# Attention scores from high and low parts: three fp32r products in place of one fp32 product

## The chip, the core and the metric

The kernel runs on one core of a Trainium2 chip. The metric is device time in microseconds (us), the median of three runs. The engines are TensorE (PE in the profile; PEld is its loading of weights), VectorE (DVE), ScalarE (ACT), GpSimd (POOL) and SyncE (SP), which here only issues transfers. Each engine works through its own list of instructions in order, and waits on semaphores for the others.

## The reference

Two layers are computed over 256 + 512 = 768 tokens (a prompt and a sample, which do not see each other) of width 1024. In each layer a projection `h @ w_in` feeds two mixers with four heads each: a gated linear attention (HGRN2, called gla in the kernel) and a differential attention. Their outputs go through a projection, a convolutional feed-forward part and a gated embedding. The change is in the scores of the differential attention:

```
q = apply_rope(q, cos, sin) * (DA_DH ** -0.5)      # DA_DH = 64, two maps m per head
k = apply_rope(k, cos, sin)
def block(q_blk):                                  # 128 queries
    s = jnp.einsum('bhmqd,bhmkd->bhmqk', q_blk, k).astype(jnp.float32)
    p = jax.nn.softmax(s, axis=-1)
    a = p[:, :, 0] - lam * p[:, :, 1]
    return jnp.einsum('bhqk,bhkv->bhqv', a.astype(v.dtype), v)
```

## The kernel before

All data are fp32. The large products (projections, feed-forward) are already made as three fp32r products: an operand x is split into a high part, which ACT writes by a copy from fp32 to fp32r, and a low part, x minus high, which DVE writes, and PE adds high x high, high x low and low x high in PSUM (`PASSES = ((0, 0), (0, 1), (1, 0))`). The small products of the two mixers are plain fp32 products.

Every engine's order is written out by hand; a `Steps` object counts named steps on a semaphore, and `done(...)` or `wait_ge(...)` waits for one. A head of both mixers is one pass `it` (eight passes: 0 to 3 in the first layer, 4 to 7 in the second). In `mixers(L, h)` PE goes through seven levels k of the gla; between them stand the attention of query block k (`att_scores`, `att_turn_weights`, `att_values`) and pieces of the projection that fill the time (`side(s)`; the table `SLOTS` says how many eighths of a projection unit stand at each place s).

Six query blocks q make a pass. Blocks 0 and 1 belong to the prompt and meet 256 keys, blocks 2 to 5 meet 512. A head has two maps m of 64 features each. Map 0 lies on partitions 0 to 63 of the tile QK, map 1 on 64 to 127, so a score step is two products of 64 rows, into two PSUM banks. QK holds queries (index 0) and keys (index 1) of all 768 tokens; QKs is a copy with the halves exchanged, for the rotation (rope). DVE makes the rotated QK in three steps of 1536 columns: `cqk` and `sqk` (multiplications, L1743) and `radd` (their sum, L1740).

The turn from one head to the next is where the change's new steps stand. PE ends the gla output of pass `it` (L1021), goes through `side(TAIL + 2)` (lines L1088), the first gla step of the next pass (L942) and the scores of its block 0 (L1041), then `side(TAIL + 3)`, then transposes of the gla output (L1027), then `side(TAIL + 4)`. `SLOTS` gives these three places 2, 0, 2 eighths after heads 0 and 2, and 1, 1, 2 after head 1; there is no turn after head 3. Meanwhile ACT squares the gla output (L2697) and merges keys (L2448); DVE copies that output (L1727, L1729), sums the squares (L1731), waits for POOL, which makes the norm from them (`ms`, L2282, and the power `rs`, L2284), scales the output (step `on`, L1807), reduces the scores of block 0 (L1748) and makes the gla queries (L1678). PE's transposes L1027 wait for `on`. The chain that starts there goes on through the gated output (L1816), ACT's high part of the next weights (L2368), DVE's low part (L1509), the gla keys (L1691), to ACT's copy of the turned weights (L2653), for which PE's first value product L1060 of the pass waits.

At the start of a layer there is no such turn: block 0 of head 0 stands in the middle of projection unit 14, after its fourth eighth.

Of the kernel before, what the change touches and what calls it, by code (L numbers as in the profile page):

```python
# [22 lines left out]
P = 128  # L23
# [7 lines left out]
NH = 4  # L31
# [95 lines left out]
def view(ap, offset, dims):  # L127

    return bass.AP(tensor=ap.tensor, offset=ap.offset + offset, ap=[list(ap.ap[0])] + [list(d) for d in dims])
# [110 lines left out]
def att_names():  # L240

    act, dve, pe = ["nb0", "e0_0", "e0_1"], ["mx0", "rc0", "lr0", "al0"], ["sc0"]
    for k in range(NT + 1):
        if k + 1 < NT:
            pe += [f"sc{k + 1}"]
            dve += [f"{x}{k + 1}" for x in ("mx", "rc", "lr", "al")]
        pe += [f"tra{k}", f"av{k}"] if k < NT else []
        act += ([f"oc{k - 1}"] if k else []) + ([f"nb{k + 1}", f"e{k + 1}_0", f"e{k + 1}_1"] if k + 1 < NT else []) + ([f"at{k}"] if k < NT else [])
    pe += ["tro0", "tro1"]
    act += ["sq", "ab0", "ab1"]  # L250
    dve += ["ss", "on"]
    return act, dve, pe


def build(nc, x_in, p_in, w_in, lb_logits, gnorm, lam_in, subln, w_a, w_b, w_out, n_mix_pre, n_mix_post,
          w_up, conv_p, w_down, n_ffn_pre, n_ffn_post, w_ple, w_ple_gate, n_ple, ident_in, masks_in,
          rope_in, out):
    with ExitStack() as ctx:
# [84 lines left out]
        for l in range(1, NL + 1):  # L343
            totals.append((TOT, sum(2 * (T >> k) for k in range(1, l))))
        QK, QKs, PR, At = stack(x_off, h_off, [
            ("QK", [P, 2, T], F32), ("QKs", [P, 2, T], F32), ("PR", [P, 2, 2, TS], F32), ("At", [P, 2, TS], F32)])
        SQ2 = view(At[:], 0, [[P, NT], [1, P]])
        ab2 = view(O2[:], 0, [[1, T]])
        HN = put("HN", [P, KD, T], F32, m_off)[0]
# [78 lines left out]
        def steps(name, names, credit=False):  # L428
            return Steps(sem(name), names, len(names) if credit else 0)
# [13 lines left out]
        G_tro = steps("gla_turned", ["tro0", "tro1"])  # L443
        G_pool = steps("gla_pool", ["ms", "rs"])
        A_rope = steps("att_rope", ["cqk", "sqk", "radd"])
        ta, td, tp = att_names()
        A_act, A_dve, A_pe = steps("att_act", ta), steps("att_dve", td), steps("att_pe", tp)
        A_pool = steps("att_pool", ["ms", "rs"])
# [360 lines left out]
        def _(pe):  # L809
# [221 lines left out]
            def att_scores(it, q):  # L1031
                k0, kn = SEQ_OF[q]
                if q == 0:
                    pe.wait_ge(A_rope.sem, A_rope.at(it, "radd"))
                    if it:
                        pe.wait_ge(A_act.sem, A_act.at(it - 1, "ab1"))
                else:
                    pe.wait_ge(A_act.sem, A_act.at(it, f"e{q - 1}_1"))
                for m in range(2):
                    rows_ = slice(m * DA_DH, (m + 1) * DA_DH)  # L1040
                    ins = mm(ps[:, AB[m], 0:kn], QK[rows_, 0, q * P:(q + 1) * P], QK[rows_, 1, k0:k0 + kn], start=True, stop=True)  # L1041
                ins.then_inc(*A_pe.step(f"sc{q}"))

            def att_turn_weights(it, q):
# [412 lines left out]
        def _(dve):  # L1457
# [267 lines left out]
            def gla_output(it):  # L1725
                done(G_pe, it, "o")
                v.tensor_copy(O1[:, 0:4, :], view(ps[:], GB[0] * 512, [[P, 4], [1, P]])).then_inc(*G_out.step("o0"))  # L1727
                done(G_sq, it, "sq1")
                v.tensor_copy(O1[:, 4:NT, :], view(ps[:], GB[1] * 512, [[P, NT - 4], [1, P]])).then_inc(*G_out.step("o"))  # L1729
                done(G_sq, it, "sq")  # L1730
                v.tensor_reduce(st_g[:, 0, :], SQ1[:], AX_X, ALU.add).then_inc(*G_out.step("ss"))  # L1731

            def att_rope(it, L, n):
# [7 lines left out]
                else:  # L1741
                    src, tab = (QK, 0) if n == "cqk" else (QKs, T)
                    v.tensor_tensor(src[:], src[:], view(rope[:], tab, [[0, 2], [1, T]]), ALU.mult).then_inc(*A.step(n))  # L1743

            def att_max(it, n):
                A, p = A_dve, n % 2
                done(A_pe, it, f"sc{n}")
                v.tensor_reduce(mx[:, p, :], ps[:, AB[0]:AB[0] + 2, 0:SEQ_OF[n][1]], AX_X, ALU.max, negate=True).then_inc(*A.step(f"mx{n}"))  # L1748
# [16 lines left out]
            def mixers(L, h):  # L1765
# [4 lines left out]
                    for j in side_splits(h, s):  # L1770
                        low(unit(L, j))

                def att_first(it):
                    att_max(it, 0)
                    att_weights(it, 0)

                if h == 0:
                    att_first(it)
                side(PRE)
                for k in range(NL):  # L1780
                    level_up_keys(it, k)
# [19 lines left out]
                if following:  # L1801
                    gla_keys(it + 1)
                    att_rope(it + 1, L, "radd")
                gla_output(it)
                done(G_pool, it, "rs")
                done(G_out, it, "o")
                v.tensor_tensor(O1, O1, view(st_g[:], 2 * NT, [[1, NT], [0, P]]), ALU.mult).then_inc(*G_out.step("on"))  # L1807
# [15 lines left out]
            for L in range(DEPTH):  # L1823
# [57 lines left out]
                v.tensor_scalar(sl_col[:], sl_col[:], lay_now[:, 1:2], None, ALU.mult).then_inc(*lay_dve.step("slw"))  # L1881
                gla_forget(L * NH)
                gla_keys(L * NH)
                gla_queries(L * NH)
                low(unit(L, DENSE))
                for h in range(NH):
                    mixers(L, h)
                for c in range(KD):
# [468 lines left out]
        def _(act):  # L2357
# [98 lines left out]
            def att_exponentials(it, n):  # L2456
# [8 lines left out]
                for m in range(2):  # L2465
                    a(PR[:, p, m, 0:kn], ps[:, AB[m], 0:kn], ACT.Exp, bias=nb[:, p, m:m + 1], scale=DA_DH ** -0.5,
                      accum_out=sm[:, p, m:m + 1]).then_inc(*A_act.step(f"e{n}_{m}"))

            def exponential_table(it):
                if it:  # L2470
                    done(A_table, it - 1, "in")
                a(exp_ahead[:], half_neg[:, 0:1], ACT.Exp).then_inc(*A_table.step("in"))
# [144 lines left out]
            def mixers(L, h):  # L2617
# [78 lines left out]
                done(G_out, it, "o0")  # L2696
                a(SQ1[:, 0:4, :], view(ps[:], GB[0] * 512, [[P, 4], [1, P]]), ACT.Square).then_inc(*G_sq.step("sq"))  # L2697
                if following:
                    merge_keys(it + 1, 0)
                exponential_table(it)  # L2700
                side(TAIL + 2)
# [62 lines left out]
            for L in range(DEPTH):  # L2764
# [67 lines left out]
                in_copy(L, I1 - 1, "c21")  # L2832
                in_store_rest(L, I1 - 1)
                load_v(L, 0)
                high(unit(L, I1 + 1))
                copy_out(L, I1, 0, (0, 7))
                store_out(L, I1, 0)
# [499 lines left out]
```

## Time and profile before

| what | before |
|---|---|
| median of 3 runs | 2427.83 us (2427.82 to 2428.07) |
| profiled execution, from the first to the last instruction (span) | 2426.0 us |
| PE busy | 2413.1 us (99%) |
| PEld busy | 2251.7 us (93%) |
| DVE busy | 1825.9 us (75%) |
| ACT busy | 1302.4 us (54%) |
| POOL busy | 195.1 us (8%) |
| mean granted clock of TensorE | 0.999 of full speed |
| DMA, mean | 133 GB/s |

A matmul's record begins when PE takes it up and ends when its result is out, so records overlap, and a busy PE is not yet a PE at its peak; what a matmul costs in a row of them is the distance from start to start. The profile has only the span of its execution; the runs' median lies 1.83 us above it, for what comes before the first instruction and after the last.

### The profile page before, as it was taken

How to read it: one execution, taken by the hardware profiler on the slowest of the kernel's cores; microseconds unless marked ns; L12 is line 12 of the kernel's file. 1: busy time of each engine (PE TensorE's matmuls, PEld its weight loads, DVE VectorE, ACT ScalarE, POOL GpSimd, SP SyncE). 2: the span in 40 equal slices, each digit the busy share in tenths (PEclk: the TensorE clock that was granted, in tenths of full speed). 3: DMA queues.
4: the chain of work that ended last, by engine and by line, in shares of the span. 5: the costliest groups of instructions: out<-in, count | busy, mean ns of one | idle time of the engine just before them, and what ended most of it. 6: DMA issues, size and time to landing. Idle time of an engine off the chain costs nothing.

```text
span 2426.0 us, 40808 instructions
## 1 busy us (share of the span) xinstructions
PE 2413.1 (99%) x16410; PEld 2251.7 (93%) x16410; DVE 1825.9 (75%) x2403; ACT 1302.4 (54%) x2014; POOL 195.1 (8%) x236
## 2 busy tenths in 40 slices
PE   9999999999999999999999999999999999999998
PEld 9999989998999999888899998899989999998887
DVE  6666777754888998978585567777649889999784
ACT  6444666543555556556454456665436555554563
POOL 0001011100200000003110011011002000000031
PEclk9999999999999999999999999999999999999999
DMA  5454444344323233833233544343443232346421
GB/s 179 138 179 135 137 138 146 117 169 150 105 72 100 84 103 108 300 114 130 97 128 125 179 148 133 128 140 126 173 148 109 68 90 84 109 155 252 153 95 61
DMA packets 290411, 321.52 MB, mean 133 GB/s; under 512 B 10416, under 2 KB 223920, under 8 KB 290224
## 3 DMA queue, kind: packets, MB, share of 16 engines
q1 hardware_dynamic: 215744, 171.39, 22.7%
q10 hardware_dynamic: 74480, 147.53, 16.8%
q8 instruction: 131, 2.15, 0.4%
q14 instruction: 56, 0.46, 0.1%
HBM read 253.60 MB, written 65.27 MB: 131 GB/s over the span
## 4 chain that ended last, share of the span: by engine, by line
PE 96%; ACT 2%; issue 1%; DVE 1%; POOL 0%; ACTq 0%; DVEq 0%; POOLq 0%
PE ps L863 23%; PE ps L1143 14%; PE ps L1325 13%; PE ps L1088 9%; PE ps L836 6%; PE ps L1431 5%; PE ps L1071 5%; PE ps L1294 3%; PE ps L1261 3%; PE ps L850 3%; PE ps L1041 2%; PE ps L915 1%; PE ps L1411 1%; PE ps L1060 1%; PE ps L972 1%
## 5 line engine op out<-in xcount | busy, mean ns | idle before, releaser
L2048 DVE TENSOR_TENSOR wlo<-raw,whi 128x1024 fp32r<-128x1024 f32 (+1 forms) x152 | 163.9, 1079 | 54.8 <-ACT whi L3018 54.8
L863 PE MATMUL ps<-hT_hi,whi 128*128 128x384 f32 x608 | 203.1, 334 | 0.0
L863 PE MATMUL ps<-hT_hi,wlo 128*128 128x384 f32 x608 | 203.1, 334 | 0.0
L863 PE MATMUL ps<-hT_lo,whi 128*128 128x384 f32 x608 | 203.1, 334 | 0.0
L3032 ACT ACTIVATE U<-ps 128x384 f32<-128x384 f32 x152 | 74.8, 492 | 223.2 <-PE ps L863 223.2
L1325 PE MATMUL ps<-whi,PH_hi 128*128 128x512 f32 x456 | 179.0, 393 | 0.0
L1325 PE MATMUL ps<-whi,PH_lo 128*128 128x512 f32 x456 | 177.6, 390 | 0.0
L1325 PE MATMUL ps<-wlo,PH_hi 128*128 128x512 f32 x456 | 177.5, 389 | 0.0
L1509 DVE TENSOR_TENSOR wlo<-raw,whi 128x2048 fp32r<-128x2048 f32 x53 | 121.9, 2301 | 69.2 <-ACT whi L2368 69.2
L1637 DVE TENSOR_TENSOR wlo<-raw,whi 128x1024 fp32r<-128x1024 f32 (+1 forms) x98 | 102.8, 1069 | 79.3 <-ACT whi L2536 79.3
L863 PE MATMUL ps<-S_hi,whi 128*128 128x384 f32 x456 | 152.3, 334 | 0.0
L863 PE MATMUL ps<-S_hi,wlo 128*128 128x384 f32 x456 | 152.3, 334 | 0.0
L863 PE MATMUL ps<-S_lo,whi 128*128 128x384 f32 x456 | 152.3, 334 | 0.0
L3018 ACT ACTIVATE whi<-raw 128x1024 fp32r<-128x1024 f32 (+1 forms) x152 | 142.1, 937 | 15.1 <-PE ps L915 14.8
L1088 PE MATMUL ps<-hT_hi,whi 128*128 128x384 f32 x512 | 136.7, 347 | 0.3 <-ACT hn L2489 0.3
L2955 ACT ACTIVATE PH_hi<-prod 128x768 fp32r<-128x768 f32 (+1 forms) x82 | 65.2, 798 | 128.5 <-PE ps L1325 104.0
L1088 PE MATMUL ps<-hT_lo,whi 128*128 128x384 f32 x512 | 130.6, 336 | 0.0
L1088 PE MATMUL ps<-hT_hi,wlo 128*128 128x384 f32 x512 | 130.5, 335 | 0.0
L1143 PE MATMUL ps<-IS_hi,whi 128*128 128x384 f32 x384 | 128.3, 334 | 0.0
L1143 PE MATMUL ps<-IS_hi,wlo 128*128 128x384 f32 x384 | 128.3, 334 | 0.0
L1143 PE MATMUL ps<-IS_lo,whi 128*128 128x384 f32 x384 | 128.3, 334 | 0.0
L2368 ACT ACTIVATE whi<-raw 128x2048 fp32r<-128x2048 f32 x53 | 101.5, 1915 | 42.6 <-PE ps L850 20.2
(333 smaller groups left out, 6999.6 us busy)
## 6 DMA issues: line engine op xcount, KB each, us to landing
raw<-w_up_dram SPq DMA_DIRECT2D x88, 512.0 KB
raw<-w_in_dram SPq DMA_DIRECT2D x64, 512.0 KB
raw<-w_down_dram SPq DMA_DIRECT2D x60, 512.0 KB, 4.7
raw<-w_in_dram SPq DMA_DIRECT2D x16, 1024.0 KB
zT<-gst ACTq DMA_DIRECT2D x40, 384.0 KB, 2.4
GT<-zT ACTq DMA_DIRECT2D x16, 768.0 KB, 5.9
pD<-CG ACTq DMA_DIRECT2D x26, 384.0 KB, 2.3
zT<-hn ACTq DMA_DIRECT2D x48, 192.0 KB, 1.9
```

What stands on the lines that cost most here:

```text
L836: ins = mm(ps[:, bank, c0:c0 + TH], W[b][:, s, w0:w0 + P], rhs[a][:, k, th * TH:(th + 1) * TH], start=(i == 0), stop=(i == n - 1))
L863: ins = mm(ps[:, 4 * (j % 2) + bank, 0:TH], quarter(L, W[y], j, (w,))[:, 0, k * P:(k + 1) * P], sum_operand(a, x, k), start=(opens and k = ...
L1071: ins = mm(o, hT[x][:, k, t * P:(t + 1) * P], view(W[y][:], w[3] * ISLOTS + k * P, [[1024, 2], [1, P]]), start=(k == 0 and i == 0), stop=( ...
L1088: ins = mm(ps[:, bank, c0:c0 + TH], W[y][:, w[3], w0:w0 + P], hT[x][:, k, th * TH:(th + 1) * TH], start=(k == 0 and i == 0), stop=(k == KD ...
L1143: ins = mm(ps[:, 4 * (e % 2) + bank, 0:TH], in_quarter(L, W[y], e, (w,))[:, 0, k * P:(k + 1) * P], in_operand(a, x, k), start=(opens and k ...
L1325: ins = mm(ps[:, FIRST_BANK[q] + t, :], ph_slot(a, n)[:, k, t * P:(t + 1) * P], view(W[b][:], ring_at(L, n) + k * 512, [[1, 512]]), start= ...
L1431: ins = mm(ps[:, t, :], gate_tokens(a, 4 * u + k, t), W[b][:, w[3], k * 512:(k + 1) * 512], start=(u == 0 and k == 0 and q == 0), stop=(u ...
L1509: v.tensor_tensor(wlo[:, g, :], raw[:, s, :], whi[:, g, :].bitcast(F32), ALU.subtract)\
L1637: v.tensor_tensor(in_quarter(L, wlo, e, names), in_raw(e, names), in_quarter(L, whi, e, names).bitcast(F32), ALU.subtract)\
L2048: v.tensor_tensor(lo, x, hi.bitcast(F32), ALU.subtract)\
L2368: a(whi[:, g, :], raw[:, s, :], ACT.Copy).then_inc(w_hi, 1)
L3018: a(hi, x, ACT.Copy).then_inc(*((w_hi, 1) if part == "T3N4" else q_hi.step(f"{part}{j}")))
```

## The change

The rotated QK is split like the operands of the large products. ACT gets a step `hi` (`att_high`): a copy of QK, 128 x 1536, into QK_hi, which lies where QKs was. DVE gets a step `lo` (`att_low`): QK minus QK_hi into QK_lo, which lies on QK itself. A score step is now six fp32r products of 64 rows, map 0 and map 1 in turn, for high x high, high x low, low x high. PE's scores of block 0 wait for `lo` in place of `radd`. At a turn `hi` stands on ACT behind the squares of the gla output, and `lo` on DVE between the sum of the squares and `on`. At the start of a layer `hi` stands behind the loads of the values and `lo` between the gla keys and the gla queries, and DVE's low part of unit 15 (`low(unit(L, DENSE))`) moves from before the first maximum of the scores to behind it.

```diff
--- before.py
+++ after.py
@@ -344,6 +344,8 @@
             totals.append((TOT, sum(2 * (T >> k) for k in range(1, l))))
         QK, QKs, PR, At = stack(x_off, h_off, [
             ("QK", [P, 2, T], F32), ("QKs", [P, 2, T], F32), ("PR", [P, 2, 2, TS], F32), ("At", [P, 2, TS], F32)])
+        QK_hi = put("QK_hi", [P, 2, T], F32R, x_off + 2 * T * 4)[0]
+        QK_lo = put("QK_lo", [P, 2, T], F32R, x_off)[0]
         SQ2 = view(At[:], 0, [[P, NT], [1, P]])
         ab2 = view(O2[:], 0, [[1, T]])
         HN = put("HN", [P, KD, T], F32, m_off)[0]
@@ -443,6 +445,8 @@
         G_tro = steps("gla_turned", ["tro0", "tro1"])
         G_pool = steps("gla_pool", ["ms", "rs"])
         A_rope = steps("att_rope", ["cqk", "sqk", "radd"])
+        A_high = steps("att_keys_high", ["hi"])
+        A_low = steps("att_keys_low", ["lo"])
         ta, td, tp = att_names()
         A_act, A_dve, A_pe = steps("att_act", ta), steps("att_dve", td), steps("att_pe", tp)
         A_pool = steps("att_pool", ["ms", "rs"])
@@ -1031,14 +1035,17 @@
             def att_scores(it, q):
                 k0, kn = SEQ_OF[q]
                 if q == 0:
-                    pe.wait_ge(A_rope.sem, A_rope.at(it, "radd"))
+                    pe.wait_ge(A_low.sem, A_low.at(it, "lo"))
                     if it:
                         pe.wait_ge(A_act.sem, A_act.at(it - 1, "ab1"))
                 else:
                     pe.wait_ge(A_act.sem, A_act.at(it, f"e{q - 1}_1"))
-                for m in range(2):
-                    rows_ = slice(m * DA_DH, (m + 1) * DA_DH)
-                    ins = mm(ps[:, AB[m], 0:kn], QK[rows_, 0, q * P:(q + 1) * P], QK[rows_, 1, k0:k0 + kn], start=True, stop=True)
+                parts = (QK_hi, QK_lo)
+                for i, (x, y) in enumerate(PASSES):
+                    for m in range(2):
+                        rows_ = slice(m * DA_DH, (m + 1) * DA_DH)
+                        ins = mm(ps[:, AB[m], 0:kn], parts[x][rows_, 0, q * P:(q + 1) * P], parts[y][rows_, 1, k0:k0 + kn],
+                                 start=(i == 0), stop=(i == 2))
                 ins.then_inc(*A_pe.step(f"sc{q}"))
 
             def att_turn_weights(it, q):
@@ -1742,6 +1749,11 @@
                     src, tab = (QK, 0) if n == "cqk" else (QKs, T)
                     v.tensor_tensor(src[:], src[:], view(rope[:], tab, [[0, 2], [1, T]]), ALU.mult).then_inc(*A.step(n))
 
+            def att_low(it):
+
+                done(A_high, it, "hi")
+                v.tensor_tensor(QK_lo[:], QK[:], QK_hi[:].bitcast(F32), ALU.subtract).then_inc(*A_low.step("lo"))
+
             def att_max(it, n):
                 A, p = A_dve, n % 2
                 done(A_pe, it, f"sc{n}")
@@ -1770,12 +1782,10 @@
                     for j in side_splits(h, s):
                         low(unit(L, j))
 
-                def att_first(it):
+                if h == 0:
                     att_max(it, 0)
+                    low(unit(L, DENSE))
                     att_weights(it, 0)
-
-                if h == 0:
-                    att_first(it)
                 side(PRE)
                 for k in range(NL):
                     level_up_keys(it, k)
@@ -1802,6 +1812,8 @@
                     gla_keys(it + 1)
                     att_rope(it + 1, L, "radd")
                 gla_output(it)
+                if following:
+                    att_low(it + 1)
                 done(G_pool, it, "rs")
                 done(G_out, it, "o")
                 v.tensor_tensor(O1, O1, view(st_g[:], 2 * NT, [[1, NT], [0, P]]), ALU.mult).then_inc(*G_out.step("on"))
@@ -1881,8 +1893,8 @@
                 v.tensor_scalar(sl_col[:], sl_col[:], lay_now[:, 1:2], None, ALU.mult).then_inc(*lay_dve.step("slw"))
                 gla_forget(L * NH)
                 gla_keys(L * NH)
+                att_low(L * NH)
                 gla_queries(L * NH)
-                low(unit(L, DENSE))
                 for h in range(NH):
                     mixers(L, h)
                 for c in range(KD):
@@ -2465,6 +2477,11 @@
                 for m in range(2):
                     a(PR[:, p, m, 0:kn], ps[:, AB[m], 0:kn], ACT.Exp, bias=nb[:, p, m:m + 1], scale=DA_DH ** -0.5,
                       accum_out=sm[:, p, m:m + 1]).then_inc(*A_act.step(f"e{n}_{m}"))
+
+            def att_high(it):
+
+                done(A_rope, it, "radd")
+                a(QK_hi[:], QK[:], ACT.Copy).then_inc(*A_high.step("hi"))
 
             def exponential_table(it):
                 if it:
@@ -2696,6 +2713,7 @@
                 done(G_out, it, "o0")
                 a(SQ1[:, 0:4, :], view(ps[:], GB[0] * 512, [[P, 4], [1, P]]), ACT.Square).then_inc(*G_sq.step("sq"))
                 if following:
+                    att_high(it + 1)
                     merge_keys(it + 1, 0)
                 exponential_table(it)
                 side(TAIL + 2)
@@ -2832,6 +2850,7 @@
                 in_copy(L, I1 - 1, "c21")
                 in_store_rest(L, I1 - 1)
                 load_v(L, 0)
+                att_high(L * NH)
                 high(unit(L, I1 + 1))
                 copy_out(L, I1, 0, (0, 7))
                 store_out(L, I1, 0)
```

PE, in the middle of the first layer's head 0, where block 2 is scored (L1060 is the value product ahead of it, L972 the gla level behind it; the waits are names of semaphores). Before:

```order
L1060 MATMUL ps<-vD,At 128x128 [waits att_v_loaded,att_act]
L1060 MATMUL ps<-vD,At 128x128
L1041 MATMUL ps<-QK 128x512 [waits att_act]
L1041 MATMUL ps<-QK 128x512
L972 MATMUL ps<-QP,KM_101 32x32 [waits gla_dve,gla_act]
```

Now:

```order
L1067 MATMUL ps<-vD,At 128x128 [waits att_v_loaded,att_act]
L1067 MATMUL ps<-vD,At 128x128
L1047 MATMUL ps<-QK_hi 128x512 [waits att_act]
L1047 MATMUL ps<-QK_hi 128x512
L1047 MATMUL ps<-QK_lo,QK_hi 128x512 x2
L1047 MATMUL ps<-QK_hi,QK_lo 128x512 x2
L976 MATMUL ps<-QP,KM_101 32x32 [waits gla_dve,gla_act]
```

Two products have become six, at the same place and behind the same wait.

DVE, at the turn from head 0 to head 1 of the first layer, from `radd` to the gla queries. Before:

```order
L1740 TENSOR_TENSOR QK<-QK,QKs 128x1536 [waits att_rope]
L1727 COPY AX<-ps 128x512 [waits gla_pe]
L1729 COPY AX<-ps 128x256 [waits gla_squares]
L1731 TENSOR_REDUCE st_g<-AT 128x6 [waits gla_squares]
L1807 TENSOR_TENSOR AX<-AX,st_g 128x768 [waits gla_output,gla_pool]
L1748 TENSOR_REDUCE mx<-ps 128x2 [waits att_pe]
L1678 TENSOR_TENSOR QP<-Qb,F 128x1536 [waits gla_pe,gla_forget]
```

Now:

```order
L1747 TENSOR_TENSOR QK<-QK,QKs 128x1536 [waits att_rope]
L1734 COPY AX<-ps 128x512 [waits gla_pe]
L1736 COPY AX<-ps 128x256 [waits gla_squares]
L1738 TENSOR_REDUCE st_g<-AT 128x6 [waits gla_squares]
L1755 TENSOR_TENSOR QK_lo<-QK,QK_hi 128x1536 [waits att_keys_high]
L1819 TENSOR_TENSOR AX<-AX,st_g 128x768 [waits gla_output,gla_pool]
L1760 TENSOR_REDUCE mx<-ps 128x2 [waits att_pe]
L1685 TENSOR_TENSOR QP<-Qb,F 128x1536 [waits gla_pe,gla_forget]
```

The step `lo` (L1755) has come in ahead of `on` (L1819), and what follows `on` stands behind both.

ACT at the same turn, the squares of the gla output and what follows them. Before:

```order
L2695 ACTIVATE AT<-ps 128x256 [waits gla_pe]
L2697 ACTIVATE AT<-ps 128x512 [waits gla_output]
L2448 ACTIVATE KM_99<-KS 128x768 [waits gla_keys]
L2472 ACT_TABLE_LOAD
```

Now:

```order
L2712 ACTIVATE AT<-ps 128x256 [waits gla_pe]
L2714 ACTIVATE AT<-ps 128x512 [waits gla_output]
L2484 ACTIVATE QK_hi<-QK 128x1536 [waits att_rope]
L2460 ACTIVATE KM_99<-KS 128x768 [waits gla_keys]
L2489 ACT_TABLE_LOAD
```

The step `hi` (L2484) starts when L2714 is through, and everything behind it on ACT moves back by its length.

## Rows read from the trace of the kernel before

**Rows 1.** The page: its span, and the engines of the chain that ended last.

```profile
span 2426.0 us, 40808 instructions
...
PE 96%; ACT 2%; issue 1%; DVE 1%; POOL 0%; ACTq 0%; DVEq 0%; POOLq 0%
```

**Rows 2.** Waits of PE: who was waited for, us in total, times, longest.

```profile
PE ps L1060 <- ACT At L2653: 2.3, 2, 1.2
...
PE ps L972 <- ACT AT L2454: 0.6, 2, 0.3
```

**Rows 3.** Source view of the scores' line: shortest, median, longest record in ns.

```profile
L1041 PE MATMUL ps<-QK x192: 376/589/693, 240.0 to 1672.2; 64*128 64x512 f32 x128, 64*128 64x256 f32 x64
```

**Rows 4.** Timeline of PE, pass 1 (start us, length us, idle before in brackets).

```profile
312.56 0.70 PE L1041 MATMUL ps<-QK 64*128 64x256 f32 x4
313.19 0.72 PE L972 MATMUL ps<-QP,KM 128*32 128x32 f32 x48
...
319.61 0.71 PE L1060 MATMUL ps<-vD,At 128*128 128x128 f32 x4 [1.13 <-ACT At L2653]
320.25 0.70 PE L1041 MATMUL ps<-QK 64*128 64x512 f32 x2
320.78 0.60 PE L1041 MATMUL ps<-QK 64*128 64x512 f32 x2
...
321.31 0.63 PE L972 MATMUL ps<-QP,KM 128*32 128x32 f32 x48
```

**Rows 5.** The chain in order of time: fp32r products of 256 and 512 columns.

```profile
249.29 5.76 PE ps L1071 x48
...
1154.18 5.46 PE ps L1431 x24
```

**Rows 6.** Groups by form, ACT and DVE, 1536 columns (busy us, mean ns).

```profile
L2438 ACT ACTIVATE F<-FZ 128x1536 f32<-128x1536 f32 x8 | 11.9, 1487 | 0.1
...
L1740 DVE TENSOR_TENSOR QK<-QK,QKs 128x1536 f32<-128x1536 f32 x8 | 14.0, 1753 | 0.1
```

**Rows 7.** Timelines of ACT and PE, turn from head 1 to head 2.

```profile
368.53 1.19 ACT L2448 ACTIVATE KM<-KS 128x768 f32<-128x768 f32 x1
...
369.87 0.70 PE L1041 MATMUL ps<-QK 64*128 64x256 f32 x4
372.70 0.49 PE L1027 MATMUL ps<-ident,AX 128*128 128x128 f32 x3
```

**Rows 8.** Timelines of ACT, POOL, DVE and PE, turn from head 0 to head 1.

```profile
303.46 1.20 ACT L2448 ACTIVATE KM<-KS 128x768 f32<-128x768 f32 x1
...
305.04 1.33 POOL L2284 TENSOR_TENSOR st_g<-st_g,half_neg 128x6 f32<-128x6 f32 x1
...
306.40 0.96 DVE L1807 TENSOR_TENSOR AX<-AX,st_g 128x768 f32<-128x768 f32 x1 [1.85 <-POOL st_g L2284]
307.67 0.69 DVE L1748 TENSOR_REDUCE mx<-ps 128x2 f32<-128x512 f32 x1 [0.31 <-PE ps L1041]
...
306.93 0.70 PE L1041 MATMUL ps<-QK 64*128 64x256 f32 x4
307.56 0.87 PE L1027 MATMUL ps<-ident,AX 128*128 128x128 f32 x6
```

**Rows 9.** Timelines of DVE and POOL: POOL's `ms` beside a DVE step, and alone.

```profile
292.69 1.75 DVE L1743 TENSOR_TENSOR QKs<-QKs,rope 128x1536 f32<-128x1536 f32 x1
...
292.97 1.53 POOL L2282 TENSOR_SCALAR st_t<-st_t 128x6 f32<-128x6 f32 x1 [50.01 <-DVE st_t L1793]
...
304.75 0.21 POOL L2282 TENSOR_SCALAR st_g<-st_g 128x6 f32<-128x6 f32 x1 [8.42 <-DVE st_g L1731]
```

**Rows 10.** Timelines of DVE and PE, start of the first layer's head 0.

```profile
236.44 1.47 DVE L1671 TENSOR_TENSOR KM<-KS 128x768 f32<-128x768 f32 x1
...
239.96 0.70 PE L1041 MATMUL ps<-QK 64*128 64x256 f32 x4
...
248.55 0.37 PE L972 MATMUL ps<-QP,KM 128*32 128x32 f32 x16 [0.28 <-ACT AT L2454]
```

## The prediction

> **What bounds the kernel now.** I read the page first: in its span of 2426.0 us PE makes 96% of the chain that ended last [rows 1], so a microsecond that PE saves is saved, and one that PE waits is lost. The waits of PE come next. PE waits only a few times for anyone, and the two that matter here come twice each, so once in a layer: a value product L1060 for ACT's copy At, 1.2 us at the longest, and a gla step L972 for AT [rows 2]. Then the scores' own line and the timeline around one step. A score step of 512 keys is four records, in two pairs: the first pair starts at 320.25, the second 0.53 us later, and the next work 0.53 us after that, so a step takes 1.06 us; one of 256 keys takes 0.63 [rows 4]. The 256 more columns cost 0.43 us in two pairs, so a pair streams 256 columns in 0.213 and 512 in 0.427 us. What remains, 0.21 us, is the same for both sizes. Half of it is in front: the first records are 104 ns longer than the second (693 against 589 ns [rows 3]), the loading of the first weights. The other half is behind. So the second pair's weights are loaded under the first pair. The two maps of a pair run side by side: four records one after the other would take 4 x 0.427 us, more than the step has.
>
> **PE's products.** No row shows fp32r products of 64 rows. Those of 128 rows come every 5.46 / 24 = 0.2275 us at 512 columns and every 5.76 / 48 = 0.120 us at 256 [rows 5]; bare streaming at twice the columns per time of the fp32 pair above would be 0.213 and 0.107. I take the measured pace for a pair, and bare streaming as the lower bound, since the fp32 pairs come at bare streaming. A step of 512 keys then changes by 3 x 0.2275 - 2 x 0.427 = -0.171 us (bound -0.213), one of 256 by 3 x 0.120 - 2 x 0.213 = -0.067 us (bound -0.107); loading in front and the change of shape behind stay. With four and two steps in each of eight passes that is 6.5 us gross. The upper bounds are below, as rivals: maps one after the other, or weights not loaded under the pair ahead.
>
> **The two new steps.** `hi` and `lo` have 1536 columns, as an ACT step of 1487 ns and a DVE step of 1753 ns have now [rows 6]. ACT is at 54% and DVE at 75%, so eight of each cost nothing by their length; they cost by where they stand. Each turn gives `lo`, ready, as the start of ACT's L2448 now, plus 1.49, plus 0.03 for the semaphore, plus 1.75, plus some 0.1 until PE starts.
>
> *Start of a layer.* DVE's gla keys end at 236.44 + 1.47 = 237.9 [rows 10]; `lo` behind them ends at 239.7, and PE wants it at 239.96. No wait, and block 0 saves 0.07. The queries, the maximum and the moved low part of unit 15 (2048 columns, 2.3 us by rows 6) are through by 245; PE takes up that unit after the step at 248.55. There PE waits 0.28 us for ACT's AT, which hangs on the projection before it, so block 1's saving goes into this wait.
>
> *Turn from head 1 to head 2.* L2448 starts at 368.53 [rows 7], so `lo` is ready at 371.9. PE, which has one eighth of a unit to do at this place and not two, is at the scores at 369.87. It waits 2.0 us, and behind it in its order stand `side(TAIL + 3)`, the transposes and all of the next pass. Nothing gives this back: +2.0 - 2 x 0.067 = +1.87 us. The transposes then come at about 374.6 and find `on` done.
>
> *Turn from head 0 to head 1.* L2448 starts at 303.46 [rows 8]: `hi` to 304.95, `lo` from 304.98 to 306.73, ready at 306.8. PE arrives at 306.93, just late enough. But POOL's `rs` starts at 305.04, inside `lo`. What that does is seen at another place: POOL's `ms` takes 0.21 us alone, and 1.53 us where a DVE step of two SBUF inputs and 1536 columns runs from 292.69 to 294.44; it ends 0.06 us after that step [rows 9]. `lo` is such a step. So I take `rs` to be held until 0.15 us before `lo` ends, and its 1.33 us then to end at 306.73 - 0.15 + 1.33 = 307.9. `on` (0.96 us) ends at 308.9 in place of 307.36, and PE's transposes start at 309.0 in place of 307.56. Behind `on` on DVE stands the maximum of the scores, which used to wait 0.31 us for PE until 307.67 and now starts at 308.87: +1.2 us. From there goes the chain of DVE and ACT steps to the copy At, for which PE waited 1.13 us at 319.61 [rows 4]. PE gets there 1.44 - 0.07 = 1.4 us later and still waits: the turn costs +1.2 us, and blocks 0 and 1 save nothing.
>
> The Trainium skill, "SBUF — State Buffer", section "Who interferes with whom", says that a DVE instruction with two SBUF inputs contends with a GpSimd instruction that reads SBUF, and that issue order decides who blocks. The trace agrees where DVE is first (1.53 for 0.21 us). By that rule a POOL step that starts first would not be held, which is the first rival below.
>
> *Turn from head 2 to head 3.* The same slots as 0 to 1, and its rows repeat rows 8 to within 0.1 us. The transposes start 1.44 us later, block 1 saves 0.07, and the chain to At (+1.2) is now behind PE: +1.4 us.
>
> **The sum**, for a layer: 16 x -0.171 = -2.74 for the blocks 2 to 5; -0.07; +1.2; +1.87; +1.4. Together +1.66 us, for two layers +3.3. The profiled span would be 2429.3, and the median, 1.83 us above the span, **2431.2 us** (+0.14%).
>
> **Rivals.** *POOL is first.* The margin is 0.06 us: if `hi` takes 1.55 us, or POOL has read its six columns by 304.98, `rs` is not held. Then `on` ends 0.3 us later, the maximum still has its slack, the turns cost 0 and +0.1, and the layer comes to -2.74 - 0.07 + 0 + 1.87 + 0.1 = -0.84: 2426.1. For it: POOL starts each `rs` about when `lo` starts. Against: in all turns my `lo` is ahead, by 0.05 to 0.13 us.
>
> *The maps don't run side by side.* Six products would come at 0.2275: a step of 512 changes by 6 x 0.2275 - 0.853 = +0.512, one of 256 by +0.293; a layer by 8.2 + 0.3 + 1.2 + 2.6 + 1.8 = +14.1, so 2456. This is the slower side: it decides from the point where three pairs take more than 0.853 us. Against it: the fp32 pairs overlap, and the new order names map 0 and map 1 in turn. For it: no fp32r row of this shape.
>
> *Weights not loaded under the pair ahead.* Each pair then takes 0.104 + 0.213 us: a step of 512 is 3 x 0.317 + 0.1 = 1.05, no gain, and one of 256 is 0.73 (+0.1). A layer comes to 0.1 + 1.2 + 2.2 + 1.6 = +5.1: 2438. Against it: the second records are 104 ns shorter than the first. The Trainium skill, "TensorE: Matmul & The Clock Gate", section "Part 3: Packing small matmuls — row/col tiling", says that weight loads overlap running matmuls only when the row group differs; by that rule this rival is the outcome. The trace disagrees for fp32 (589 against 693 ns), and no run here shows fp32r.
>
> *No wait at head 1 to 2.* If `lo` came in time there too, the layer would be -0.84 - 1.87 - 0.13 = -2.8, so 2422. It needs `hi` and `lo` to take 1.2 us together, against 3.24 in the rows.
>
> **Chances and range.** Forecast 0.55, POOL first 0.20, serial maps 0.13, loads not hidden 0.06, no wait 0.06. A measurement of this kernel can tell some 0.2% (4.9 us) from no change, so 2423.0 to 2432.7 counts as the same. "Same" is POOL first and all of the forecast but 0.08 (should the three turns cost 0.3 us more each, or the pairs come 0.03 us later): 0.67. Slower: 0.08 + 0.06 + 0.13 = 0.27. Faster: 0.06. The range reaches from POOL first with bare streaming (-3.41 - 0.11 + 0 + 1.79 + 0.07 = -1.66 in a layer: 2424.5) to the loads that are not hidden (2438.0); it leaves out the serial maps and the last rival, together 0.19.
>
> **What would show it.** Right: score steps of about 0.89 and 0.57 us, three pairs 0.23 us apart; PE waiting for `lo` 2.0 us twice, in no other turn; `rs` of 2.9 us at the turns, and PE waiting for `on` four times, about 1.5 us each. Wrong: a score step over 1.06 us; `rs` still 1.33 us; PE waiting for `lo` at heads 0 to 1 or 2 to 3, or at a layer's start.

## The result, and the profile after

The changed kernel takes **2434.53 us** (median of 7 runs, 2432.54 to 2437.61) against 2427.89 for the kernel before on the same chip (7 runs, 2427.80 to 2428.26): ratio 1.003, 95% interval 1.002 to 1.004. It is slower by 6.6 us, or 0.27%, a little more than the 0.2% that a measurement can tell. The forecast was 2431.2: right in sign, 3.3 us short. Its runs also lie 5 us apart, those of before 0.5. The profiled execution took 2434.52 us.

The page of the changed kernel answers to [rows 1]; below it PE's waits, which answer to [rows 2]:

```profile
span 2432.7 us, 41016 instructions
...
PE 93%; DVE 2%; ACT 2%; issue 1%; POOL 1%; DMA 1%; SPq 0%; ACTq 0%; POOLq 0%; DVEq 0%
```

```profile
PE ps L1031 <- DVE AX L1819: 5.9, 4, 1.5
PE ps L1047 <- DVE QK_lo L1755: 4.0, 2, 2.1
PE ps L1067 <- ACT At L2670: 2.8, 2, 1.4
...
PE ps L976 <- ACT AT L2466: 0.8, 2, 0.4
```

Two waits are new, and both come from the split: four times 1.5 us for the normalised gla output (`on`, the transposes of AX), and twice about 2 us for `lo`. The wait for At grew from 1.2 to 1.4 us.

A score step of 512 keys in the timeline of PE (start us, length us), for [rows 4]:

```profile
387.61 0.50 PE L1047 MATMUL ps<-QK_hi 64*128 64x512 f32 x2
387.94 0.39 PE L1047 MATMUL ps<-QK_lo,QK_hi 64*128 64x512 f32 x2
388.18 0.40 PE L1047 MATMUL ps<-QK_hi,QK_lo 64*128 64x512 f32 x2
388.50 0.63 PE L976 MATMUL ps<-QP,KM 128*32 128x32 f32 x48
...
387.71 0.19 PEld L1047 LDWEIGHTS ps<-QK_lo,QK_hi 64*128 64x128 f32 x2
387.95 0.19 PEld L1047 LDWEIGHTS ps<-QK_hi,QK_lo 64*128 64x128 f32 x2
```

Three pairs start within 0.57 us, and the step takes 0.89 us in place of 1.06. The second pair starts 0.33 us behind the first, and the third 0.24 us behind the second, little more than the 0.2275 us of one such product of 128 rows in [rows 5]. So the two maps run side by side. The weights of the second and the third pair are loaded (PEld) while the pair ahead still runs.

The turn from head 0 to head 1 in the timelines of ACT, DVE, POOL and PE, for [rows 8]:

```profile
302.93 1.48 ACT L2484 ACTIVATE QK_hi<-QK 128x1536 fp32r<-128x1536 f32 x1
...
304.44 1.76 DVE L1755 TENSOR_TENSOR QK_lo<-QK,QK_hi 128x1536 fp32r<-128x1536 f32 x1 [0.42 <-ACT QK_hi L2484]
...
304.50 2.89 POOL L2296 TENSOR_TENSOR st_g<-st_g,half_neg 128x6 f32<-128x6 f32 x1
...
307.42 0.96 DVE L1819 TENSOR_TENSOR AX<-AX,st_g 128x768 f32<-128x768 f32 x1 [1.22 <-POOL st_g L2296]
308.90 2.65 DVE L1685 TENSOR_TENSOR QP<-Qb,F 128x1536 f32<-128x1536 f32 x1
...
308.46 1.47 POOL L2324 TENSOR_TENSOR TOT<-F 128x768 f32<-128x768 f32 x1 [1.07 <-DVE AX L1819]
...
308.44 0.88 PE L1031 MATMUL ps<-ident,AX 128*128 128x128 f32 x6 [1.49 <-DVE AX L1819]
```

`lo` starts 0.06 us ahead of `rs`, ends at 306.20, and `rs` ends 1.19 us later: 2.89 us for a step that took 1.33.

Behind `on` come POOL's first total and DVE's gla queries QP. The same two steps before:

```profile
307.44 1.47 POOL L2312 TENSOR_TENSOR TOT<-F 128x768 f32<-128x768 f32 x1 [1.07 <-DVE AX L1807]
...
308.28 2.25 DVE L1678 TENSOR_TENSOR QP<-Qb,F 128x1536 f32<-128x1536 f32 x1
```

The turn from head 1 to head 2 on PE, for [rows 7], and behind it windows of that time in both layers (start and end us, length, then busy time of PE, PEld, DVE, ACT and POOL, the granted clock, DMA share, GB/s):

```profile
372.21 0.39 PE L1047 MATMUL ps<-QK_hi 64*128 64x256 f32 x2 [1.91 <-DVE QK_lo L1755]
...
372.76 1.01 PE L1095 MATMUL ps<-hT_hi,whi 128*128 128x384 f32 x2
373.57 0.84 PE L1095 MATMUL ps<-hT_hi,wlo 128*128 128x384 f32 x2
...
377.51 0.51 PE L1095 MATMUL ps<-hT_hi,wlo 128*128 128x384 f32 x2
```

```profile
370.00:372.20 2.20, 0.30 (x33) 0.19 (x19) 1.76 (x1) 2.18 (x3) 1.94 (x2) 1.00 0.01 4
372.20:376.40 4.20, 4.19 (x18) 4.05 (x19) 3.03 (x3) 2.67 (x8) 3.05 (x3) 0.59 0.02 4
376.40:380.00 3.60, 3.60 (x25) 3.56 (x24) 3.53 (x7) 1.93 (x1) 3.29 (x5) 1.00 0.89 284
1577.00:1579.20 2.20, 0.16 (x16) 0.05 (x5) 1.78 (x2) 2.18 (x3) 1.89 (x2) 1.00 0.00 1
1579.20:1583.00 3.80, 3.74 (x26) 3.58 (x27) 2.59 (x4) 2.45 (x7) 2.65 (x2) 1.00 0.00 0
```

PE stands idle for 1.91 us, and then the same products that take 0.51 us a pair at 377.51 take 0.84: the granted clock of that stretch is 0.59, so it is mostly the lower level, 1.2 GHz (from 372.80 to 376.10 it is 0.50). Matched record by record with the execution of before, PE loses 1.5 us more between 372.76 and 376.13. In the second layer a wait of 2.1 us at the same place is followed by a clock of 1.00. So one execution holds both outcomes.

### The profile page after: what moved, and what is told of

Its sections match the earlier page's. It is cut to its first block, busy times and chain, and to the rows that moved or that the text cites. A ratio compares the mean times of both kernels' runs of the same rounds, so it can differ in the third digit from the quotient of the medians.

```text
span 2432.7 us, 41016 instructions
## 1 busy us (share of the span) xinstructions
PE 2408.1 (99%) x16506; PEld 2259.5 (93%) x16506; DVE 1840.9 (76%) x2411; ACT 1312.7 (54%) x2022; POOL 207.5 (9%) x236
## 4 chain that ended last, share of the span: by engine, by line
PE 93%; DVE 2%; ACT 2%; issue 1%; POOL 1%; DMA 1%; SPq 0%; ACTq 0%; POOLq 0%; DVEq 0%
PE ps L867 23%; PE ps L1150 14%; PE ps L1332 13%; PE ps L1095 8%; PE ps L840 5%; PE ps L1438 5%; PE ps L1078 5%; PE ps L1301 3%; PE ps L1268 3%; PE ps L854 3%; PE ps L919 1%; PE ps L1418 1%; PE ps L1047 1%; PE ps L1067 1%; PE ps L976 1%
```

## The experiments

Ratios are taken against runs of the kernel before on the same chip (medians 2427.81 to 2427.88 us).

**The two halves of the change apart.** First the products without the split:

```diff
-                parts = (QK_hi, QK_lo)
+                parts = (QK_lo, QK_lo)        # QK_lo: the sum itself, as fp32r
...
-                    att_high(it + 1)          # hi, lo and their waits: all gone
...
-                    att_low(it + 1)
```

> Three fp32r products a step as in the change, but with no split: the first and the second operand are the sum itself, read as fp32r, in all three products, so the high and the low step on ACT and DVE, their waits and the moved split of the dense unit are all gone (the scores come out three times too large: the low parts are left out). Theory (the products gain, the two new steps at the turns lose): the trace of the changed kernel shows 0.90 us for a 512-key step and 0.55 for a 256-key step, 0.16 and 0.075 less than before; 16 and 8 of them a layer give 3.2 us a layer, so about 2421.7 us (2421 to 2423.5), and the turns look as before. Rival (the steps' gain is not on the path, or a product in three parts costs the steps as much as it saves): 2427 to 2428.

Then the split with the old products:

```diff
-                        ins = mm(ps[:, AB[m], 0:kn], parts[x][rows_, 0, q * P:(q + 1) * P], parts[y][rows_, 1, k0:k0 + kn],
-                                 start=(i == 0), stop=(i == 2))
+                    ins = mm(ps[:, AB[m], 0:kn], QK_hi[rows_, 0, q * P:(q + 1) * P].bitcast(F32), QK_hi[rows_, 1, k0:k0 + kn].bitcast(F32), start=True, stop=True)
```

> The high and the low step with their waits as in the change, but two plain fp32 products a step, of the high parts alone (the low parts are computed and not used). Theory: the turns cost what the trace of the changed kernel shows, 1.5 us at the turn from head 0 to 1, 1.9 at 1 to 2, 1.5 at 2 to 3, that is 4.9 a layer, and 0 to 1.5 us a layer for a clock that falls after the longest wait: 2437.6 to 2441 us, with the spread of the changed kernel. Rival (the turns wait because the new products bring PE there earlier, and with the old products most of it is covered): 2428 to 2432.

Measured: 2422.47 us for the products (11 runs, ratio 0.9979, 0.9970 to 0.9988) and 2439.62 for the split (5 runs, 1.0048, 1.0035 to 1.0061). That is -5.3 and +11.8 us, together +6.5; the change measured +6.6. So the halves add up (to 0.1 us by luck: the runs of the change lie 5 us apart, those of the split 3), and each rival falls: the products do gain on the path, and the turns wait whatever the products are. The waits of the split alone, the rows of its trace:

```profile
PE ps L1031 <- DVE AX L1816: 5.5, 4, 1.4
PE ps L1045 <- DVE QK_lo L1752: 3.8, 2, 1.9
```

The products gave 0.8 us less than the expected 2421.7. PE's wait for At is 1.4 us there too: a part of what the first two steps of a head save goes into that wait.

**Is `rs` held, or is `on` only behind `lo`?** A small reduction on DVE lets POOL's `rs` start first:

```diff
+                    done(G_pool, it, "ms")
+                    v.tensor_reduce(dly[:], gT[:, it % 2, 0:256], AX_X, ALU.add)
                     att_low(it + 1)
```

> The changed kernel with one thing more: ahead of the low step DVE waits for POOL's ms and then reduces 256 columns of gT into one unused column, so that POOL's rs starts before the low step does; the low step itself starts and ends some 0.5 us later. Theory (rs is held because DVE's two-operand step has the port when rs comes to read): rs is back at 1.3 to 1.5 us (2.88 in the changed kernel), the six transposes of AX at the turns 0 to 1 and 2 to 3 wait 0.3 to 0.6 us in place of 1.47, scores at 1 to 2 wait 0.5 us longer than their 1.9 to 2.1; 4 times -1.0 and 2 times +0.5: 2430 to 2432.5 us. Rival (the normalised output is late because it stands behind the low step on DVE, or POOL is slowed for as long as they overlap whoever came first): rs stays over 2.2 us, every turn is 0.3 to 0.5 us later, 2436 to 2439 us.

Measured: 2434.08 us (10 runs, 2431.83 to 2437.05; 1.0026, 1.0017 to 1.0035), between the theory and the rival: 0.45 less than the change, which runs 5 us apart cannot tell from nothing, and not the 2 to 4.5 expected. But in its trace the mechanism is there: first `rs` (source view, shortest, median, longest in ns), then the timelines of POOL and DVE at the turn from head 0 to 1, then PE's waits:

```profile
L2299 POOL TENSOR_TENSOR st_g<-st_g,half_neg x8: 1320/1322/1330, 304.8 to 1707.3; 128x6 f32<-128x6 f32 x8
```

```profile
304.80 1.33 POOL L2299 TENSOR_TENSOR st_g<-st_g,half_neg 128x6 f32<-128x6 f32 x1
...
305.09 1.75 DVE L1756 TENSOR_TENSOR QK_lo<-QK,QK_hi 128x1536 fp32r<-128x1536 f32 x1
```

```profile
PE ps L1048 <- DVE QK_lo L1756: 5.5, 6, 2.4
...
PE ps L1032 <- DVE AX L1822: 1.0, 4, 0.3
```

`rs` takes 1.32 us again although `lo` runs beside it, and PE's waits for `on` fall from 5.9 to 1.0 us. So the hold is shown, and so is that the order of the two starts decides it. The Trainium skill says in "SBUF — State Buffer", section "Who interferes with whom", that issue order decides who blocks. For `rs` the traces agree: 2.88 us with DVE ahead, 1.32 with POOL ahead. That the second one would be blocked the other way round they don't show: `lo`, started second, keeps its 1.75 us beside an `rs` that runs for another 1.04. The gain didn't reach the time for two reasons. `lo` comes later: the waits at head 1 to 2 are 2.4 us in both layers (1.9 and 2.1 in the change), and at the other turns four waits of 0.2 us for `lo` are new. And the slow stretch now stands behind the wait at head 1 to 2 in both layers.

**What the clock costs.** Products of the identity with itself keep PE busy during the wait at head 1 to 2:

```diff
+                    if h == 1:
+                        pe.wait_ge(A_act.sem, A_act.at(it, "ab1"))
+                        for _ in range(16):           # 8 in the second version
+                            mm(ps[:, AB[2], 0:P], ident[:], ident[:], start=True, stop=True)
                     att_scores(it + 1, 0)
```

> The changed kernel with sixteen products of the identity with itself (128 columns, plain fp32, into a bank that is free) on PE at the turn from head 1 to 2, ahead of the wait for the low step; they write what nobody reads. Theory (the clock falls because PE stands idle there for 2 us; the wait itself costs what it costs): the scores start at the same time as before, the products of the dense units behind them come every 0.17 us in every layer, and the time is the best of the changed kernel's runs: 2431.5 to 2433 us, with a spread below 1.5 us in place of 5. Rival (the clock falls for another reason, by time or by what runs elsewhere): 2433.5 to 2436 us, spread as before.

> The kernel in which rs starts before the low step, with twenty-one of the same products of the identity on PE at the turn from head 1 to 2. Its trace showed the transposes of AX waiting 0.3 us in place of 1.5, scores at 1 to 2 waiting 2.4 us in place of 2, and a slow clock behind that wait in both layers. Theory (what the freed rs gave was eaten by the clock): without the slow stretch the gain of the products, 5.4 us, stands against 0.5 + 2.6 + 0.5 us of waits in each of two layers: 2429 to 2431 us, spread below 1.5 us. Rival (the freed rs gives nothing on the path): 2432 to 2435 us.

Both were too long: I had taken 0.11 us for such a product, and it takes two records, 0.24 us. PE's timeline in the first:

```profile
370.09 3.84 PE L1141 MATMUL ps<-ident 128*128 128x128 f32 x32
373.86 0.39 PE L1047 MATMUL ps<-QK_hi 64*128 64x256 f32 x2
```

So PE came some 1.7 us late to the scores (373.86 against 372.21 in the change), and the times miss theory and rival alike and decide nothing: 2436.22 us (1.0034, 1.0021 to 1.0047) for sixteen, 2435.71 (1.0033, 1.0020 to 1.0046) for twenty-one with `rs` first. The spread does say something: 0.5 us in five runs of the sixteen, 1.3 in five of the twenty-one. With the count mended:

> The changed kernel with eight products of the identity on PE ahead of the wait for the low step at the turn from head 1 to 2. With sixteen they ran for 3.8 us (0.24 us each), 1.9 us longer than the wait, and the time was 2436.2 us with a spread of 0.5 us; eight run for 1.9 us, no longer than the wait. Theory (the clock falls because PE stands idle): 2 times 1.9 us less than with sixteen, 2432.4 us (2432 to 2433.2), spread below 1.5 us. Rival (the slow stretches come back, or the sixteen helped by something else): 2433.5 to 2436 us, spread 3 us or more.

> The kernel in which rs starts before the low step, with ten products of the identity on PE at the turn from head 1 to 2 (2.4 us, no longer than the wait there; with twenty-one they ran for 4.9 us, and it took 2435.71 us). Theory (what the freed rs gave was eaten by the clock): 2 times 2.4 us less, 2430.9 us (2430 to 2431.5), spread below 1.5 us, against 2434.08 without the products. Rival (the freed rs gives nothing on the path): 2432 to 2435 us.

Measured: 2432.78 us for eight (11 runs, 2432.63 to 2433.88; 1.0021, 1.0012 to 1.0029), 2430.25 for ten with `rs` first (11 runs, 2429.90 to 2430.82; 1.0010, 1.0002 to 1.0019). Both are as the theory had them. Windows of the eight, at the same times as those of the change:

```profile
370.00:372.20 2.20, 2.20 (x46) 2.04 (x33) 1.76 (x1) 2.18 (x3) 1.98 (x2) 1.00 0.04 11
372.20:376.40 4.20, 4.20 (x30) 4.03 (x30) 3.07 (x3) 2.64 (x9) 3.05 (x3) 1.00 0.00 0
```

The scores start at 372.17, as in the change at 372.21: nothing of the wait is gone, only PE's idleness. The clock stays at 1.00, and median and spread fall by 1.75 and 3.8 us. So idleness ahead of it is what brings the slow clock on. What it is worth differs from run to run: 1.75 us of the median of seven runs that lie between 0.2 us below and 4.8 us above the 2432.78, and 1.5 us in the execution that was profiled. With the clock held, `rs` first is worth 2432.78 - 2430.25 = 2.5 us.

The traces, one execution of each kernel, say how often it falls. Of the waits at head 1 to 2 that nothing fills, two each in the change (1.9 and 2.1 us), the split alone (1.9 both) and `rs` first (2.4 both), five of six are followed by a slow stretch. Behind the 22 waits of 1.4 to 1.5 us for `on` in five traces (the change, the split alone, eight and sixteen products, and the next experiment) there is none.

**PE later at the turn.** One entry of the table of side work:

```diff
-SLOTS = (..., (0, 2, 2, 2, 2, 2, 2, 1, 1, 0, 1, 1, 2),
+SLOTS = (..., (0, 2, 2, 2, 2, 2, 2, 1, 1, 0, 2, 0, 2),
```

> The changed kernel with one number moved in the table of side work: at the turn from head 1 to 2 both pieces of the dense units stand ahead of the first scores, as at 0 to 1, in place of one ahead and one behind. Theory: PE comes to the scores 3.5 us later, so these wait for nothing; then the transposes of AX wait 1.5 us as at the other turns, because rs is still held: 0.4 to 0.6 us a layer less wait, and no slow stretch since no wait is as long as 2 us: 2432 to 2433.5 us, spread below 2 us. Rival (any wait of 1.5 us can bring the slow clock, or the piece ahead is itself waited for): 2434 to 2437 us.

Measured: 2432.92 us (11 runs, 2431.58 to 2434.00; 1.0020, 1.0011 to 1.0029). As expected: the waits for `lo` are gone, and two more for `on` have come in their place. The spread of 2.4 us is a little more than expected. The trace, which is of the fastest of these runs, has no slow stretch; whether the clock falls behind the waits of 1.5 us in others stays open.

```profile
PE ps L1031 <- DVE AX L1819: 8.7, 6, 1.5
```

**The split where there is room.** The first two score steps of a head read only the first 256 tokens. So the sum, `hi` and `lo` are made in two parts:

```diff
+        NEW = {"0": slice(0, TP), "": slice(TP, T)}
...
+                    att_rope(it + 1, L, "radd0")      # DVE, ahead of the gla keys
                     gla_keys(it + 1)
...
+                    att_low(it + 1, "0")              # ACT's hi of it: ahead of the copy x8s
                 gla_output(it)
...
+                    if q == 2:
+                        pe.wait_ge(A_low.sem, A_low.at(it, "lo"))
```

> The change with the split made in two parts: the sum, the high and the low step for the first 256 tokens (all that the first two score steps of a head read) ahead of the gated head's output, in idle time of ACT and DVE, and those of the other 512 tokens later, before the third score step; at two turns the second rope product moves into DVE's idle time before the last query step. Theory (the loss is in the turns' waits alone, and nothing of it is inherent in three products): rs takes 1.3 us again, the transposes of AX wait as before (0.1 to 0.3 us), scores wait for nothing, and the gain of the products stays: 2421.5 to 2424 us. Rival (DVE is full between the turns, so the moved parts come back as waits of the level steps and of the weights' transposes): 2425 to 2429 us.

Measured: 2436.36 us (5 runs, 1.0034, 1.0021 to 1.0047): the rival, and worse than it. The waits at the turns are gone, but others have come, by this trace's waits of PE and ACT's timeline:

```profile
PE ps L1098 <- ACT hn L2522: 7.3, 4, 3.5
PE ps L1070 <- ACT At L2686: 4.9, 4, 1.5
```

```profile
377.42 1.06 ACT L2500 ACTIVATE QK_hi<-QK 128x1024 fp32r<-128x1024 f32 x1 [4.49 <-DVE QK L1751]
...
378.66 1.91 ACT L2395 ACTIVATE whi<-raw 128x2048 fp32r<-128x2048 f32 x1 [0.18 <-issue]
380.47 0.79 ACT L2522 ACTIVATE hn<-ps 128x768 f32<-128x768 f32 x1
```

I had put the late `hi` at head 1 to 2 where ACT's queue stood 4.5 us for DVE's late sum, and behind it were two steps that PE needs. Again the products behind that wait came at 0.32 us in place of 0.17: from 380.50 to 387.30 the granted clock is 0.50. The second version mends the two places:

```diff
+                if h == 1:                             # in the time of POOL's rs
+                    done(G_pool, it, "ms")
+                    v.tensor_reduce(dly[:], gT[:, it % 2, 0:256], AX_X, ALU.add)
+                    att_rope(it + 1, L, "radd")
...
-                    if h == 2 and k == 0:
+                    if h >= 2 and k == 0:
                         att_low(it, "")
```

> The split in two parts again, with the late part mended where the first version put new waits: at the turn from head 1 to 2 the late sum stands in DVE's idle time while POOL's rs runs (behind a small reduction, so that rs starts first) and its high step in ACT's idle time ahead of the first exponentials, where the first version held up a copy that PE waited 3.5 us for; at 2 to 3 the late low step moves behind the first query step, where the first version held up a row maximum and PE 1.1 us. Theory (the waits were those of the order and no more, and the clock fell behind the long one): no wait over 0.5 us at any turn, no slow stretch, the gain of the products alone left: 2422 to 2424 us with a spread under 2 us. Rival (ACT and DVE have no room left for 3 us a turn, the wait moves to a third place): 2425 to 2430 us.

Measured: 2426.70 us (11 runs, 2425.93 to 2427.57; 0.9995, 0.9986 to 1.0004), no different from before, and between the two theories. One new wait was left, for At, 1.04 us in the first layer and 0.90 in the second (4 waits in place of 2):

```profile
PE ps L1071 <- ACT At L2689: 4.5, 4, 1.4
```

The third puts the late `lo` at head 2 to 3 into the time of `rs` as well:

```diff
-                    if h >= 2 and k == 0:
+                    if h == 2 and k == 0:
...
-                if h == 1:
+                if h in (1, 2):
...
-                    att_rope(it + 1, L, "radd")
+                    if h == 1:
+                        att_rope(it + 1, L, "radd")
+                    else:
+                        att_low(it + 1, "")
```

> The split in two parts, second version, with its last wait mended: there the late low step at the turn from head 2 to 3 pushed DVE's work back until PE waited 1.04 us for weights eight score steps' worth of work later, once a layer. Now it stands where the late sum stands at 1 to 2, behind the small reduction while rs runs, where DVE was idle for 1.9 us. Theory: 2 times 1.04 us less than the 2426.70 of the second version, 2424.6 us (2424 to 2425.3), which is faster than the kernel before by over 0.1%. Rival (rs is held again, or the normalised output comes late behind it): 2426 to 2428 us.

Measured: **2424.12 us** (11 runs, 2423.56 to 2424.74; ratio 0.9985, 0.9976 to 0.9994), as expected, and the only version with the split that is faster than before (by 0.15%, with an interval that excludes no change). It is 1.65 us above the products alone. Its turn from head 2 to 3 on POOL and DVE:

```profile
432.41 1.32 POOL L2317 TENSOR_TENSOR st_g<-st_g,half_neg 128x6 f32<-128x6 f32 x1 [0.17 <-POOL st_g L2315]
...
432.27 0.42 DVE L1830 TENSOR_REDUCE dly<-gT 128x1 f32<-128x256 f32 x1 [0.43 <-POOL st_g L2315]
432.61 1.22 DVE L1761 TENSOR_TENSOR QK_lo<-QK,QK_hi 128x1024 fp32r<-128x1024 f32 x1
433.76 0.96 DVE L1837 TENSOR_TENSOR AX<-AX,st_g 128x768 f32<-128x768 f32 x1
```

`rs` ends at 433.73 and `lo` at 433.83: two thirds of the step that cost PE 1.5 us at this place now cost next to nothing, and PE's waits for `on` and `lo` are gone from the trace.

## Why the prediction was right in sign and 3.3 us short

- **The score steps** were right in kind. Predicted 0.89 us at 512 keys, measured 0.89 to 0.91; predicted 0.57 at 256, measured 0.55 to 0.56. Of the rivals, maps one after the other (1.57 us a step) and weights not loaded under the pair ahead (1.05) fall. By the Trainium skill, "TensorE: Matmul & The Clock Gate", section "Part 3: Packing small matmuls — row/col tiling", weight loads overlap running matmuls only when the row group differs. The trace disagrees for fp32r as it did for fp32: all three pairs use the same two row groups, and the loads of the second and the third run from 387.71 and 387.95, under the pairs that started at 387.61 and 387.94. By the prediction's terms the products alone give -6.1 us; they gave -5.3. Matched record by record with before, a step of 512 keys saves 0.16 us in that run where 0.171 was forecast, and in the pass behind the turn from head 2 to 3 PE loses some 0.2 us a layer ahead of value products, where the forecast had it lose nothing.
- **Turn 1 to 2** was right but for the clock: 2.0 us predicted, 1.9 and 2.1 us waited in the two layers.
- **The hold of `rs`** was right, and "POOL is first" was no outcome of the change; the experiment that made POOL first shows what that is worth, 2.5 us with the clock held. The rival had been priced at 5.1 (2431.2 against 2426.1), but without the 0.3 to 0.5 us by which the experiment puts `lo` later, so that price stays untested. `on` waits of 1.5 us came four times, as forecast.
- **Turn 0 to 1** was mis-sized: +1.2 predicted; PE lost 1.41 at the transposes, got back 0.10 and lost 0.25 more at At, +1.56 (+1.57 in the second layer). The step that failed is the one that gave 0.24 us back before At. The maximum came 1.2 us later as forecast, but the next DVE step, QP (L1685), took 2.65 us in place of 2.25. POOL's first total (1.47 us) follows `on` and is still running when QP starts: for 0.63 us before (308.28 to 308.91), for 1.03 now (308.90 to 309.93), and QP is longer by just that difference. In all 16 QP steps of the two kernels, with overlaps of 0.28 to 1.03 us, QP is 1.61 to 1.62 us plus the overlap, as if it stood still until POOL is through. Turn 2 to 3 came to +1.48 in both layers (1.4).
- **The start of a layer** was wrong in a small way: no wait was predicted, and PE stood 0.1 to 0.2 us longer ahead of these scores (they start at 240.11 in the first layer, `lo` wanted at 239.96). A wait for `lo` there was among the signs of being wrong. The term that was off is the length of `lo`: priced at 1.75 us, it took 2.06 and ended at 239.96 in place of 239.7. A POOL step that began before it still ran for 0.44 us, as with QP:

```profile
237.25 1.10 POOL L2324 TENSOR_TENSOR TOT<-TOT 128x192 f32<-128x192 f32 x1
237.91 2.06 DVE L1755 TENSOR_TENSOR QK_lo<-QK,QK_hi 128x1536 fp32r<-128x1536 f32 x1
```

- **The clock** was left out of the sum: it stood there at nothing, without a reason. It is the largest part: 1.75 us of the median by the runs that kept PE busy. The products alone are 0.75 us off, the turns 0.9 (2432.78 - 2422.47 = 10.3 us, against 9.4 in the prediction's terms); together 3.4 us, where 3.3 are missing. That they add up so closely is in part luck, since the median of seven runs 5 us apart could as well have come out a microsecond higher or lower.
- **The chances** leaned the other way. All but 0.08 of the forecast stood for a time up to 2432.7, which would have counted as the same; 2434.53 lies above that, on the side that had 0.27. The forecast's sign came from -6 us of products against +9.4 of turns, and both halves came out in kind as described; its size was half of what was measured.

Why the clock fell behind one wait of 2 us in the change and not behind the other is open.

## What to carry to other kernels

An operand split costs what its place in each queue costs: the 3.2 us of `hi` and `lo` took 2 us of PE at the turn from head 1 to 2, and made in two parts at other places of the same turn they left no wait there. Look for the step that reads least of the operand, split for it first, and put the rest into time in which the engine stands waiting, behind the start of the step on another engine that it would hold up. And price an idle PE above its length where the clock can fall behind it: in the profiled executions an idle time of 1.9 us cost 1.5 us more here, and one of 2.4 us, in the second layer of the run with `rs` first, 2.8 more.

## What had not been expected of the hardware

After 1.9 us of idleness the granted clock was 0.59 over 4.2 us, after 2.1 us at the same place a layer later 1.00; after 3.5 us of waiting (the split in parts) the pace was again 0.32 us a product. The fall makes a kernel's runs differ by 5 us where those of before differ by 0.5, and those of the change with PE kept busy by 1.3. And contention goes both ways, but not with every step: a POOL step of six columns grew from 1.33 to 2.89 us under a DVE step that began 0.06 us ahead of it. DVE's QP takes 1.61 us plus the time that POOL's total, begun before it, still runs (1.90 to 2.65 us). But `lo` beside a six-column step of POOL that began 0.29 us ahead of it took 1.75 us, no more than 1536 columns take elsewhere (1753 ns in [rows 6]).
